# A two-block transformer step on one core: the router's choice, the split of the first tokens, the last expert's output and an inverse's idle gaps are rewritten

## The reference, cut to what matters

```python
# gated delta rule: per head and 64-token chunk, the inverse of a unit lower triangle
Tm = lax.linalg.triangular_solve(eye + L, eye, left_side=True, lower=True, unit_diagonal=True)
o = rmsnorm(o, norm_w) * silu(gate_b)          # gate_b: one product of the layer's input
# mixture of experts, 8 experts of width 3584, the best 2 of each token
logits = h @ router_w + router_b
top_val, top_idx = lax.top_k(logits, 2)
top_w = softmax(top_val)
for e in range(8):
    out = out + gates[..., e:e+1] * ((silu(h @ wg[e]) * (h @ wu[e])) @ wd[e])
x = x + g2 * out
return rmsnorm(x, final_norm_w)
```

## Time and profile before

| | us |
|---|---|
| median of 3 runs (lowest, highest) | 2210.45 (2207.23, 2212.51) |
| the profiled execution, by its own time | 2212.68 |
| its span in the profile | 2210.8 |
| PE busy | 2132.3 (96%) |
| DVE busy | 1729.5 (78%) |
| ACT busy | 1344.9 (61%) |
| POOL busy | 106.6 (5%) |

### The profile page before, as it was taken

How to read it: one execution, slowest core, us unless ns; L and a number is a source line. 1 busy time by engine, 2 the same in 40 slices (tenths; PEclk the granted TensorE clock), 3 DMA queues, 4 the chain that set the end, 5 groups by cost and what they waited for, 6 DMA issues and landing times.

```text
span 2210.8 us, 30652 instructions
## 1 busy us (share of the span) xinstructions
PE 2132.3 (96%) x11803; PEld 1807.8 (82%) x11803; DVE 1729.5 (78%) x1691; ACT 1344.9 (61%) x1446; POOL 106.6 (5%) x138
## 2 busy tenths in 40 slices
PE   7999999999999999999999999999999999999995
PEld 6877897789888695998897788888888888888884
DVE  7567678777755664677789888988988888988996
ACT  4754456565334423443683677777777777777874
POOL 2000000000010010101000000000000000000000
PEclk9999999999999999999999999999999999999998
DMA  8854654567877302768665799999999999999994
GB/s 318 288 191 170 221 193 157 187 221 250 288 264 254 134 30 77 281 244 297 238 230 190 281 392 365 389 366 392 363 392 365 390 368 387 373 383 381 375 392 163
DMA packets 249520, 621.27 MB, mean 281 GB/s; under 512 B 13722, under 2 KB 22293, under 8 KB 249366
## 3 DMA queue, kind: packets, MB, share of 16 engines
q1 hardware_dynamic: 229524, 530.29, 65.7%
q0 software_dynamic: 16864, 81.86, 10.4%
q10 hardware_dynamic: 3042, 7.87, 0.9%
HBM read 611.60 MB, written 12.58 MB: 282 GB/s over the span
## 4 chain that ended last, share of the span: by engine, by line
PE 81%; DVE 11%; ACT 3%; issue 2%; DMA 2%; POOL 0%; DVEq 0%; POOLq 0%; ACTq 0%
PE ps L1596 27%; PE ps L1601 14%; PE ps L723 12%; PE ps L769 9%; PE ps L750 5%; DVE ring_low L2368 3%; DVE ada L2377 2%; DVE arena L2377 2%; PE ps L825 2%; DVE arena L2368 1%; ACT arena L1642 1%; PE ps L1567 1%; PE ps L1385 1%; ACT part_high L1645 1%; PE ps L1483 1%
## 5 line engine op out<-in xcount | busy, mean ns | idle before, releaser
L3384 DVE TENSOR_TENSOR w_low<-ring,w_high 128x2048 fp32r<-128x2048 f32 x288 | 655.3, 2287 | 87.4 <-PE ps L1601 66.7
L2333 ACT CAST w_high<-ring 128x2048 fp32r<-128x2048 f32 x288 | 549.1, 1910 | 175.7 <-PE ps L1601 156.3
L1645 ACT CAST part_high<-ring 128x1024 fp32r<-128x1024 f32 x287 | 296.3, 1048 | 286.4 <-PE ps L769 114.7
L1596 PE MATMUL ps<-w_high,tokens_hl 128*128 128x512 f32 x1792 | 447.9, 392 | 2.1 <-ACT w_high L2333 2.1
L2368 DVE TENSOR_TENSOR ring_low<-ring,part_high 128x1024 fp32r<-128x1024 f32 x287 | 340.9, 1217 | 135.3 <-ACT part_high L1645 133.5
L1596 PEld LDWEIGHTS ps<-w_high,tokens_hl 128*128 128x128 f32 x1792 | 333.4, 188 | 70.6 <-ACT w_high L2333 2.6
L769 PE MATMUL ps<-part_high,arena_split 128*128 128x512 f32 x752 | 237.4, 396 | 6.1 <-issue 4.2
L1601 PE MATMUL ps<-w_low,tokens_hl 128*128 128x512 f32 x896 | 240.4, 390 | 1.2 <-DVE w_low L3384 1.2
L1596 PE MATMUL ps<-w_high,hidden_hl 128*128 128x512 f32 x896 | 224.1, 392 | 0.0
L1601 PEld LDWEIGHTS ps<-w_low,tokens_hl 128*128 128x128 f32 x896 | 168.1, 188 | 37.6 <-DVE w_low L3384 2.1
L1596 PEld LDWEIGHTS ps<-w_high,hidden_hl 128*128 128x128 f32 x896 | 166.4, 188 | 33.6
(11 more groups left out here) (303 smaller groups left out, 2433.0 us busy)
## 6 DMA issues: line engine op xcount, KB each, us to landing
ring<-in_moe_w_gate SPq DMA_DIRECT2D x96, 1024.0 KB, 7.8
ring<-in_moe_w_up SPq DMA_DIRECT2D x96, 1024.0 KB, 8.0
ring<-in_moe_w_down SPq DMA_DIRECT2D x96, 1024.0 KB, 7.0
slab<-in_ada_w POOLq DMA_DIRECT2D x64, 768.0 KB, 5.5
ring<-in_w_in SPq DMA_DIRECT2D x19, 2048.0 KB, 8.7
ring<-in_w_ff SPq DMA_DIRECT2D x16, 2048.0 KB, 8.9
hT<-in_moe_w_up SPq DMA_DIRECT2D x16, 1024.0 KB, 7.9
hT<-in_moe_w_gate SPq DMA_DIRECT2D x16, 1024.0 KB, 8.3
```

The source lines that it names most:

```text
L1596: pe.matmul(ps[:, bank, :], acts[:, x_, k0 + k, :], high[:, k, h * 512:(h + 1) * 512], start=(start and k + x_ == 0), stop=False)
L1645: L(nc.scalar.copy(o, i), s)
L2333: nc.scalar.copy(high, whole).then_inc(sem("high_ready"), 1)
L3384: V.tensor_tensor(low, whole, high.bitcast(F32), ALU.subtract).then_inc(sem("low_ready"), 1)
```

## The change

In neutral words, by place:

1. **Delta rule.** The sums of b=3 go to bank 6, the turn banks become (2, 7, 6, 4) and the product banks (3, 5, 0, 1), so that banks 3 and 5 are free for `gate_product`. That product is cut into pieces of two feature tiles: one piece ahead of `pair_products(0)`, one each behind the turns of b=1, b=2 and b=3, then token tile 1. VectorE does slab 9 together with 10 and 11, after the first inverses, and not ahead of `masked_pair(0)`.
2. **Norm of units 2 and 5.** The last half is squared ahead of `turned_odd(u, 0)`.
3. **Router.** One dummy product stands before the router products and one behind (four before the change, two of them in the middle). Experts are chosen by pairwise comparison of all eight logits. Selection 0 is built straight from the slot numbers. `vector2` 6 is announced with the round count. The rows are worked out by POOL, behind its share of the split. The table of Silu is loaded ahead of the loop.
4. **First split.** VectorE splits tiles 0 to 3, between its two `modulate` calls; POOL splits tiles 4 to 7.
5. **End.** The last round's result is not stored. POOL gathers the chosen rows (rows of the last expert replaced by others whose weight is zero) when the last hidden tile has been turned, that is during the last round's down products, weighs them and adds them to x on GpSimd, in eight operations of 128x1024. After the loop TensorE multiplies the last result by the turned selection matrix of the last round (four float32 products of 128x512), VectorE adds this to x half by half, ScalarE squares by halves, and out is stored in four transfers. The copy from HBM to HBM that pads `expert_rows` grows from 8 to 9 blocks of 128 rows.

```diff
@@ inverse, TensorE @@
+            pe.wait_ge(sem("l2_ln"), 2)
+            wt = weights("gate_b", 0)
+            gate_product(0, 0, 2)
             pair_products(0)
             decay_sums(2, 2)
-            decay_sums(3, 3)
+            pe.wait_ge(sem("dn_dec"), 1)
+            decay_sums(3, 6)
             pair_products(1)
             turn_inverse(0, 0)
             turn_inverse(0, 1)
+            gate_product(0, 2, 4)
             turn_inverse(0, 2)
-            gate_product(0)
+            gate_product(0, 4, 6)
             turn_inverse(0, 3)
-            gate_product(1)
+            gate_product(0, 6, 8)
+            gate_product(1, 0, 8)
@@ router, TensorE @@
             turn_token(5, 0)
+            stay_awake(4, 1)
...
-                        stay_awake(7, 2)
...
-            stay_awake(7, 2)
+            stay_awake(7, 1)
@@ after the loop, TensorE @@
+            pe.wait_ge(sem("selected"), n_rounds + 2)
+            for t in range(TT):
+                mm = pe.transpose(ps[:, 6, t * P:(t + 1) * P], select[:, t, :], ident)
+            mm.then_inc(sem("gathered"), 1)
+            pe.wait_ge(sem("hidden_copied"), n_rounds * GU + 1)
+            for t in range(TT):
+                for h in range(2):
+                    if t == 0:
+                        pe.wait_ge(sem("expert_out"), n_rounds * 2 + (h + 1))
+                    pe.matmul(ps[:, 2 * t + h, :], A(ESELT, TT, P)[:, t, :], A(EY + h * 512, 512), start=True, stop=True
+                              ).then_inc(lin_done, 1)
@@ norm_stage, ScalarE @@
-                        if u not in H_OF and (t, h) == (1, 1):
-                            turned_odd(u, 0)
                         act.wait_ge(sem("x_added"), 4 * (u - 1) + 2 * t + h + 1)
                         half_squares(u, t, h)
+                if u not in H_OF:
+                    turned_odd(u, 0)
@@ first split, VectorE @@
+            modulate(1, range(0, 4)).then_inc(sem("gathered_ready"), 1)
+            V.tensor_copy(tokens_hl[:, 0, 0:4], gathered[:, 0:4]).then_inc(sem("tokens_high"), 1)
+            V.tensor_tensor(tokens_hl[:, 1, 0:4], gathered[:, 0:4], tokens_hl[:, 0, 0:4].bitcast(F32), ALU.subtract
                             ).then_inc(sem("tokens_low"), 1)
+            modulate(2, range(4, 8)).then_inc(sem("gathered_ready"), 1)
@@ end, GpSimd @@
-            pool.wait_ge(sem("scalar2"), 6)
+                pool.wait_ge(sem("hidden_turned"), n_rounds * GU)
+                pool.wait_ge(sem("rows_moved"), n_rounds * 16 + 48)
             for t in range(TT):
                 for j in range(2):
...
+            for t in range(TT):
+                pool.wait_ge(sem(f"chosen{t}"), 32)
+                c0, c1 = (A(CHOICE[t][j], D) for j in range(2))
+                for j, c in enumerate((c0, c1)):
+                    L.settle()
+                    L(G.tensor_scalar(c, c, kept[:, 2 * j + t:2 * j + t + 1], None, ALU.mult))
+                L.settle()
+                L(G.tensor_tensor(c0, c0, c1, ALU.add))
+                L.settle()
+                L(G.tensor_tensor(x[:, t, :], x[:, t, :], c0, ALU.add))
@@ end, VectorE @@
+            build_selection(n_rounds - 1).then_inc(sem("selected"), 1)
             copy_output(n_rounds * E_STEPS + plan.steps, n_rounds * 16 + 48)
...
+                    stt(x[:, t, sl], ps[:, 2 * t + h, :], last_gate[:, t:t + 1], x[:, t, sl], ALU.mult, ALU.add,
+                        sem("x_final"))
```

More of the change, by code:

```diff
@@ L656, in _ @@
             slot_token = rounds[:, 2 + 2 * TT:3 + 2 * TT].bitcast(mybir.dt.uint32)
-            pool.wait_ge(sem("slot_tokens"), 1)
+            L, G = Lane(pool, sem("pool_step")), nc.gpsimd
+            ranked, over, late = small[:, 520:536], A(MO + 64, TT * EXPERTS), A(MO + 80, TT * EXPERTS)
+            picks, tops, limit = small[:, 536:568], small[:, 568:572], A(MO + 96, 1)
+            row_of_last = A(MO + 100, 4)
+            L(G.tensor_tensor(picks[:, 16:32], A(MO, TT * EXPERTS), picks[:, 0:16], ALU.subtract))
@@ new lines, in _ @@
+            L(G.tensor_scalar(over, ranked, P + 0.5, 1.0 * (EXPERTS - 1) * P, ALU.is_gt, ALU.mult))
+            L(G.tensor_scalar(late.rearrange("p (t e) -> p t e", t=2),
+                              con("eight_down").unsqueeze(1).broadcast_to([P, TT, EXPERTS]), -1.0 * P, None, ALU.mult))
+            L(G.tensor_scalar(limit, small[:, 572:573], 1.0 * P, None, ALU.mult))
+            L.settle()
+            L(G.tensor_tensor(over, over, ranked, ALU.add))
+            L.settle()
+            L(G.tensor_tensor(over, over, late, ALU.add))
@@ new lines, in _ @@
+            L.settle()
+            for j in range(2):
+                L(G.tensor_tensor(picks[:, 16 * j:16 * j + 16], picks[:, 16 * j:16 * j + 16], over, ALU.mult))
+            L.settle()
+            by_pick = picks.rearrange("p (a e) -> p a e", e=EXPERTS)
+            for step in (4, 2):
+                L(G.tensor_tensor(by_pick[:, :, 0:step], by_pick[:, :, 0:step], by_pick[:, :, step:2 * step], ALU.add))
+                L.settle()
+            L(G.tensor_tensor(tops, by_pick[:, :, 0], by_pick[:, :, 1], ALU.add))
@@ new lines, in _ @@
+            L.settle()
+            L(G.tensor_scalar(tops, tops, (EXPERTS + 1.0) * P - 1.0, None, ALU.add))
+            L.settle()
+            L(G.tensor_scalar(small[:, 504:508], tops, limit, None, ALU.is_ge))
+            L.settle()
+            L(G.tensor_scalar(row_of_last, small[:, 504:508], -1.0 * P, None, ALU.mult))
+            L.settle()
+            L(G.tensor_tensor(tops, tops, row_of_last, ALU.add))
+            L.settle()
+            L(G.tensor_copy(rounds[:, 2:2 + 2 * TT], tops))
@@ new lines, in _ @@
+            pool.wait_ge(sem("slot_tokens"), 1)
+            weight, of_last, kept, last_gate = (small[:, c:c + n] for c, n in ((574, 4), (504, 4), (508, 4), (512, 2)))
+            L(G.tensor_tensor(small[:, 576:578], small[:, 500:502], weight[:, 0:2], ALU.mult))
+            L.settle()
+            L(G.tensor_tensor(kept, weight, of_last, ALU.mult))
+            L.settle()
+            L(G.tensor_tensor(last_gate, kept[:, 0:2], kept[:, 2:4], ALU.add))
+            L.settle()
+            L(G.tensor_tensor(kept, weight, kept, ALU.subtract))
@@ L663, in _ @@
+            with pool.Fori(0, 1):
+                pool.wait_ge(sem("rows_moved"), n_rounds * 16 + 48)
             for t in range(TT):
```

203 lines of the change are left out of this document (101 added, 102 removed).

## The result

| | before | after |
|---|---|---|
| median of 20 runs each (lowest, highest), us | 2211.13 (2204.32, 2216.27) | 2208.11 (2202.87, 2211.63) |
| the profiled execution, its own time / span | 2212.68 / 2210.8 | 2208.51 / 2206.4 |
| POOL busy | 106.6 | 154.9 |

The ratio is 0.9985 with an interval of 0.9978 to 0.9992: the changed kernel is 3.3 us faster by the ratio (1.8 to 4.9) and 3.0 by the medians, where 10.9 us were forecast. This is a gain, but under the 0.2% that was called measurable. The time lies inside the stated range (2191.5 to 2209) near its slow end, outside case (A)'s own 2195 to 2204, and in the band from 2206.0 to 2214.9 that was called "same" and given 0.11.

What follows compares the result with a forecast made beforehand. TensorE was taken as the bound, busy 96% of the span, with VectorE at 90% in the loop. The terms -11.8 + 5.6 - 4.0 + 0.4 - 1.1 gave -10.9 us and a forecast of 2199.5 us, range 2191.5 to 2209.

Steps and rivals of the forecast that it cites:

- case (A): Whole kernel: the outcome as forecast, 2199.5 us, with its own range of 2195 to 2204; chance 0.47.
- the entry: Expert loop's first halves: POOL's cast waits behind one `w_low`, tokens ready at +13.1; 1.1 us saved, router's gain included.
- the end: After the loop's last product: 22.7 us shrink to 10.9 us, 11.8 us saved.
- The inverse: Delta rule: pieces of `gate_product` fill TensorE's 5.4 us of idle; 4.0 us saved, bounds 2 and 5.4.
- Unit 2's norm: Norm ahead of unit 2: odd tiles start 1.1 us later, behind the half's square; +0.4 us (0 to +1.1).
- The router: Router: earlier squaring and fewer dummies gain 1.15 + 1.88 us; after the clock's loss the gather starts 2.6 us earlier.
- an earlier fall of the clock: Router: with fewer dummies TensorE's clock falls 1 to 2 us earlier; 0.8 us lost of a possible 2.6.
- The loop's delay: Last twelve halves: POOL's eight operations, 13.2 us, slow VectorE by 7.4; less 1.8 of room, TensorE ends 5.6 us later.
- a sign that the prediction itself had named for being wrong: Last round of the loop: the prediction would be wrong if a `w_low` beside POOL stays at 2.29 us.
- rival (C): Last halves: each POOL operation holds VectorE for its whole length; 5.8 us more, 2205.3; chance 0.16.
- rival (D): Clock and blocked split eat the router's gain, weights starve at the gathers: +2.6 and +3, 2205; chance 0.10.

Runs made afterwards that it cites:

- e3: The changed kernel with the chosen rows weighed and added by VectorE, GpSimd only gathering them: 2202.85 us, ratio to before 0.9963.
- g1: e5, but GpSimd weighs and adds token tile 0's chosen rows in the last round: 2201.48 us, ratio to before 0.9951.
- e5: The changed kernel with both halves of the first split and the chosen rows' arithmetic done by VectorE: 2194.76 us, ratio to before 0.9925.
- e1: The changed kernel with the first split as before, GpSimd on tiles 0 to 3 and VectorE on 4 to 7: 2202.26 us, ratio to before 0.9959.
- h1: g1 with only GpSimd's two multiplications for tile 0, the additions by VectorE after the loop: 2198.80 us, a single run.
- h2: g1 with only GpSimd's two additions for tile 0, its rows unweighted: 2198.54 us, a single run.
- e4: The changed kernel with GpSimd's eight operations on the chosen rows held until the expert loop is over: 2217.33 us, a single run.

## Why the prediction was wrong, and which terms held

10.9 us were forecast and 3.3 measured. Two terms of the sum were off by 5.7 us together: the entry and the end.

**The inverse** was right in mechanism and size: -4.4 for -4.0. VectorE did wait 2.81 us for slab 11 (the last row above), and nothing waited for VectorE.

**Unit 2's norm**: +0.8 for +0.4, inside its bounds. I took the earlier wait of the first product group as cover; the products that wait for the odd tiles start 0.82 us later, all of it passed on.

**The router** gained more than stepped: the gather starts 22.0 us after the last `ring_low` subtraction, before 25.5, which is 3.5 us where I had 2.6 (whose own terms add up to 2.5), and it isn't longer for the clock (5.23 us for 5.28). The loss of 0.8 us to an earlier fall of the clock did not come in this trace: the 24 router products took 2.74 us, 3.36 before. It came in two of the ten traces with the new router, e3 and g1. After:

```profile
1213.61 2.74 PE L1600 MATMUL ps<-router,hT 128*128 128x8 f32 x24
1220.45 5.23 PE L1620 MATMUL ps<-arena 128*128 128x128 f32 x32
```

g1:

```profile
1211.25 4.34 PE L1593 MATMUL ps<-router,hT 128*128 128x8 f32 x24
1219.69 6.72 PE L1613 MATMUL ps<-arena 128*128 128x128 f32 x32
```

In g1 the clock is already granted at half (a mean of 0.53) from 1212 to 1214 us, where the 24 products have just begun. Against e5 this costs 1.6 us ahead of the gather and 1.3 in it. e3's rows are alike (4.53 and 6.53 us), and its gather starts 1.8 us later than the changed kernel's, as much as its "router and entry" is longer. In the changed kernel's own trace the router lost nothing to the clock, but the clock makes this stage differ between executions of equal code.

The first product of half 0 comes 4.8 us earlier (28.20 for 32.97 us after the same point). 3.5 of this is the gather. In e1, where GpSimd splits these tokens as before, it comes at 29.24, so VectorE's split is worth 1.0 of it.

**The entry is the step that failed.** The prediction put it: "I let it wait as in the loop: behind `w_low` 0 (2.29), cast 0.6, behind `w_low` 1, subtraction 1.0; tokens ready at +13.1". The cast waited for three `w_low`, not one, which stood back to back because both buffers were free and the third's was released meanwhile; tokens were ready at +15.9 (1220.45 to 1236.32). The trace of before already held this row:

```profile
1234.19 6.69 DVE L3384 TENSOR_TENSOR w_low<-ring,w_high 128x2048 fp32r<-128x2048 f32 x3
```

Three `w_low` without a pause open the loop there too; I priced the wait by how the loop runs later. The two slab additions of the earlier trace rows are 0.1 us apart (the first takes 2.39 us from 796.46, the second starts at 798.96), and GpSimd got in between them. The `w_low` at the entry leave no such pause. That this decides is argued and not tested, and e1's small operations, each let in after one `w_low`, speak against it as the whole reason. Why the cast waited for all three stays open; that it did, and what it cost, is shown.

Behind the standstill the clock fell, which the prediction looked for in the gather, ahead of the loop, but not here. Together +2.1 for -1.1; e1 and e5 show what the same router gives with a split that doesn't wait for GpSimd: 107.7 and 108.0, 4 us under before. The traces of the changed kernel and of e5 divide the 6 us between. Counted from the last `ring_low` subtraction, half 1's first product comes at 37.9 us after the change and at 34.0 in e5, half 2's at 42.7 and 36.7: 3.9 us are the wait and 2.0 the clock behind it.

Even without GpSimd in the split the stage is not always 108: of six traces with e5's code there four had 107.9 to 108.0, but g1 and h1 111.9 and 109.6. In g1 2.2 us of this is the router's clock and 1.6 eight products of half 1 at half clock. In h1, too, twelve products of halves 0 and 1 were partly at half clock, behind a standstill of 2.48 us that in e5 (2.50) was followed by none. So the clock can fall here without GpSimd.

**The loop's delay**, +5.0 for +5.6, is right in size by luck: the working is wrong. The eight operations are 20.9 us and not 13.2, the multiplications being 2.9 and not 1.2 each; VectorE lost 6.1 us and not 7.4; and no rate per us of GpSimd describes it, as g1, h1 and h2 show. What it comes to is room left, and then the clock: 5.3 us lost against some 2.5 of room where I had 1.8, and 2.2 more behind the standstill, most of it the clock, where the prediction had nothing. That `w_low` beside tile 1's multiplications stayed at 2.28 us is a sign that the prediction itself had named for being wrong. On rival (C) the rows speak for both sides. The Trainium skill ("SBUF — State Buffer", "SBUF: two separate sides") has whoever starts first hold the shared pair for its whole instruction. The additions agree (the `w_low` at 2175.47 starts 0.6 us behind one, which has 2.0 us left, and loses 1.9), the multiplications don't (0.6 us lost beside one of 2.9), and GpSimd's cast, which should have waited for one instruction of VectorE, waited for three. Of rival (D) the first term came, the entry (2.6 us above the forecast in (D), 3.2 measured); its second, weights that starve at the gathers, did not: e3 has the gathers and 39.77 us.

**The end**: -9.3 for -11.8, the second mis-sized term. From the last product, forecast and measured: to the first product 0.8 and 0.9; the products 3.5 and 3.7; the last additions 0.7 and 2.0, since they waited for GpSimd until 2197.97 and only then did both halves; squares and root 1.1 and 1.5, as ScalarE does two halves in turn; scaling 1.3 and 1.4; the store 3.0 and 3.75. e5's end, without GpSimd, is still 13.1, so some 2 us of this were plain omissions: in these traces the last token tile's two halves are always squared in turn, since what they wait for is late for both.

Of the 5.1 us between -10.9 and -5.8, the entry is 3.2, the end 2.5, the norm 0.4; the inverse and the loop give back 0.4 and 0.6. What the runs have less than the stages, 3.3 for 5.8 us, stays open.

## What to carry to other kernels

Ask of work moved to GpSimd not how long it takes but what VectorE does at that moment: behind back-to-back operations with two SBUF inputs even a small cast can wait for all of them, and whatever depends on it waits too. On a stage where the other engine has little room, price the loss against that room and not by a rate, and add the clock that TensorE may lose behind a standstill. Here VectorE, 90% busy, did the moved work for less than GpSimd, which was idle: the chosen rows took it four operations of some 1.3 us (e3), and GpSimd eight of 20.9 us in all.

## What the hardware did that was not expected

- A GpSimd cast of 128x512 took 7.01 us beside three consecutive `w_low` of VectorE (after, e3, e4), 0.61 alone; an operation of 128x1 took 2.20 beside one `w_low` (e1) and 0.22 alone (after).
- On GpSimd a multiplication of 128x1024 by a scalar for each partition takes longer (2.9 us) than an addition of two tensors of that size (2.34).
- The addition takes 1.9 us from a `w_low` of 2.29 beside it, the longer multiplication 0.6, and nothing from the last three `w_low` of the changed kernel.
- Behind a standstill of TensorE of 5.1 us at the entry, and behind two of 0.8 and 2.0 us in the last round, eight products ran at 1.2 GHz (3.77 and 3.41 us for 1.98). That the standstills cause it wasn't tested by itself, and they don't decide it alone: behind 1.4 us in h2 and 2.50 in e5 the clock stayed, behind 2.48 in h1 it fell.
